# The shared key's rotation shared between VectorE and GpSimd, and a new order of roundings ahead of the attention

## The reference

```python
def mla(cq, ckv, kr, q_norm, w_uq, kv_norm, w_ukv, cos, sin):
    q = (rmsnorm(cq, q_norm) @ w_uq).reshape(B, S, ATT_HEADS, QK_DIM)          # 8 heads of 64 + 32
    q = jnp.concatenate([q[..., :NOPE_DIM], apply_rope(q[..., NOPE_DIM:], cos, sin)], axis=-1)
    q = q * QK_DIM ** -0.5
    kv = (rmsnorm(ckv, kv_norm) @ w_ukv).reshape(B, S, ATT_HEADS, NOPE_DIM + V_DIM)
    k_nope, v = kv[..., :NOPE_DIM], kv[..., NOPE_DIM:]
    k_rope = apply_rope(kr[:, :, None, :], cos, sin)                           # one key part for all heads
    k = jnp.concatenate([k_nope, jnp.broadcast_to(k_rope, (B, S, ATT_HEADS, ROPE_DIM))], axis=-1)
    ...                                                                        # softmax(q k^T) v per head

def apply_rope(x, cos, sin):
    x1, x2 = x[..., :ROPE_DIM // 2], x[..., ROPE_DIM // 2:]
    return jnp.concatenate([x1 * c - x2 * s, x2 * c + x1 * s], axis=-1)
```

## Time and profile before

| | |
|---|---|
| median of 3 runs | 1396.53 us (1396.4 to 1396.9) |
| span of the profiled execution | 1392.5 us, mean granted TensorE clock 0.994 |
| lowest run less that span | 3.9 us |
| PE busy | 1360.1 us, 98% of the span |
| DVE, ACT, POOL busy | 879.0, 662.6, 680.1 us |
| chain that ended last | 86% on PE |

### The profile page before, as it was taken

How to read it: one execution, slowest core, us unless ns; L and a number is a source line. 1 busy time by engine, 2 the same in 40 slices (tenths; PEclk the granted TensorE clock), 3 DMA queues, 4 the chain that set the end, 5 groups by cost and what they waited for, 6 DMA issues and landing times.

```text
span 1392.5 us, 19360 instructions
## 1 busy us (share of the span) xinstructions
PE 1360.1 (98%) x6940; PEld 1123.6 (81%) x6940; DVE 879.0 (63%) x1186; ACT 662.6 (48%) x1235; POOL 680.1 (49%) x540
## 2 busy tenths in 40 slices
PE   6999999999998999999999999999999999999997
PEld 5888888878885777888888888888888888878886
DVE  7125455535686777245684565566899888895284
ACT  5323232323456876445675555545444444545452
POOL 4374636347434764454567777775300443003480
PEclk9999999999999999999999999999999999999999
DMA  5221111111222000725533333435767744674251
GB/s 204 69 70 37 31 31 31 27 31 49 58 62 68 1 1 4 254 93 165 180 108 122 121 121 106 132 95 195 266 207 239 243 134 131 233 235 156 88 183 73
DMA packets 138254, 162.10 MB, mean 116 GB/s; under 512 B 16688, under 2 KB 82224, under 8 KB 138160
## 3 DMA queue, kind: packets, MB, share of 16 engines
q1 hardware_dynamic: 138160, 160.87, 36.6%
HBM read 139.86 MB, written 18.87 MB: 114 GB/s over the span
## 4 chain that ended last, share of the span: by engine, by line
PE 86%; DVE 6%; issue 3%; POOL 2%; DMA 1%; ACT 1%; SPq 0%; DVEq 0%; POOLq 0%; ACTq 0%
PE ps L50 25%; PE ps L52 24%; PE ps L51 24%; PE ps L981 4%; PE ps L1819 2%; PE ps L1860 2%; PE ps L1631 1%; PE ps L1028 1%; PE ps L1013 1%; DVE op_low L2297 1%; DVE wy_low L2303 1%; DMA k_t<-k_rope 1%; DVE w_sum L2274 1%; PE ps L1025 1%; POOL k_low L1648 0%
## 5 line engine op out<-in xcount | busy, mean ns | idle before, releaser
L1531 POOL TENSOR_TENSOR wy_low<-w_raw,wy_high 128x512 fp32r<-128x512 f32 x107 | 159.6, 1494 | 177.9 <-ACT wy_high L1474 177.8
L50 PE MATMUL ps<-wy_high,op_high 128*128 128x512 f32 x448 | 175.0, 391 | 0.8 <-DVE op_low L2297 0.4
L51 PE MATMUL ps<-wy_low,op_high 128*128 128x512 f32 x448 | 174.3, 389 | 0.0
L52 PE MATMUL ps<-wy_high,op_low 128*128 128x512 f32 x448 | 174.3, 389 | 0.0
L381 POOL TENSOR_TENSOR wx_low<-w_raw,wx_high 128x512 fp32r<-128x512 f32 (+1 forms) x64 | 83.1, 1305 | 143.1 <-ACT wx_high L501 143.1
L1474 ACT ACTIVATE wy_high<-w_raw 128x512 fp32r<-128x512 f32 x118 | 74.4, 631 | 155.0 <-PE ps L52 151.5
L1531 POOL TENSOR_TENSOR wy_low<-t_sum,wy_high 128x512 fp32r<-128x512 f32 x64 | 89.0, 1391 | 53.8 <-ACT wy_high L1474 53.6
L1531 POOL TENSOR_TENSOR wy_low<-w_sum,wy_high 128x512 fp32r<-128x512 f32 x32 | 44.4, 1388 | 130.4 <-ACT wy_high L1474 130.3
L1474 ACT ACTIVATE wy_high<-w_sum 128x512 fp32r<-128x512 f32 x80 | 50.6, 632 | 118.7 <-PE ps L52 96.6
L50 PE MATMUL ps<-h_high,wx_high 128*128 128x512 f32 (+1 forms) x256 | 102.6, 401 | 0.0
L50 PE MATMUL ps<-a_high,wy_high 128*128 128x512 f32 x256 | 100.1, 391 | 0.0
(11 more groups left out here) (292 smaller groups left out, 3512.9 us busy)
## 6 DMA issues: line engine op xcount, KB each, us to landing
w_raw<-in_w_down SPq DMA_DIRECT2D x127, 256.0 KB, 3.3
raw_more<-in_w_down SPq DMA_DIRECT2D x65, 256.0 KB, 3.5
w_raw<-in_w_up SPq DMA_DIRECT2D x64, 256.0 KB, 3.3
w_raw<-in_w_in SPq DMA_DIRECT2D x62, 256.0 KB, 2.8
w_raw<-in_w_o SPq DMA_DIRECT2D x32, 256.0 KB, 2.7
raw_more<-in_w_up SPq DMA_DIRECT2D x32, 256.0 KB, 3.3
w_raw<-in_w_ple_gate SPq DMA_DIRECT2D x32, 256.0 KB, 2.6
keep_h<-comb SPq DMA_DIRECT2D x26, 256.0 KB, 2.2
```

Of the source, the lines that this page charges most:

```text
L50: pe.matmul(out, stat_high, mov_high, start=start, stop=False)
L51: pe.matmul(out, stat_high, mov_low, start=False, stop=False)
L52: return pe.matmul(out, stat_low, mov_high, start=False, stop=stop)
L1531: pool.tensor_tensor(low_tile, tile_raw(tile), high_tile.bitcast(F32), ALU.subtract).then_inc(low_made, 1)
```

## The change

Five things change in it, all ahead of the attention.

1. The rotation of the shared key is taken from VectorE's branch `n == 12`. VectorE makes only the shuffle, into a buffer of its own (`k_swap`), ahead of its first job. GpSimd makes the four products right behind the rests of `wq`, and the sum after its second `q_rope` sum.
2. The loads of `wkv` count on their own semaphore `wkv_loaded`; VectorE waits for six loads of `p4_loaded` instead of eight, ScalarE for the two of `wkv` only when it comes to them.
3. ScalarE takes jobs 1 and 2 ahead of rounding the last latents, and jobs 4 and 5 ahead of rounding `wkv`.
4. VectorE makes the rests of the last latents at job 6 instead of ahead of job 0, and GpSimd makes the rests of `wkv` behind its first `q_rope` sum.
5. VectorE and ScalarE each wait for `q_roped` and `k_roped` before their first `v` job, and a semaphore of one count (`q_sq_added`) is merged into another.

```diff
+            k_swap = at("k_swap", [ROPE, T], F32, scratch_at + 32768)
@@ SP
-                    sp.dma_start(wkv[:, k, :]...).then_inc(p4_loaded, 16)
+                    sp.dma_start(wkv[:, k, :]...).then_inc(wkv_loaded, 16)
...
-                sp.wait_ge(k_roped, 1)
+                sp.wait_ge(k_roped, 5)
@@ GpSimd
                 for k in range(2):
                     latent_weight_low("wq", wq, wq_high, wq_low, k)
-                for k in range(2):
-                    latent_weight_low("wkv", wkv, wkv_high, wkv_low, k)
+                pool.wait_ge(p4_loaded, 16 * 6)
+                pool.wait_ge(rope_step, 1)
+                for g in range(2):
+                    pool.tensor_tensor(k_rope[:, HALVES[g]], k_rope[:, HALVES[g]], cos[0:ROPE, :], ALU.mult).then_inc(k_roped, 1)
+                    pool.tensor_tensor(k_swap[:, HALVES[g]], k_swap[:, HALVES[g]], sin[0:ROPE, :], ALU.mult).then_inc(k_roped, 1)
...
                         pool.tensor_tensor(out, out, buf, ALU.add).then_inc(q_roped, 1)
+                        if steps_of == 1:
+                            for k in range(2):
+                                latent_weight_low("wkv", wkv, wkv_high, wkv_low, k)
+                        if steps_of == 2:
+                            pool.wait_ge(k_roped, 4)
+                            pool.tensor_tensor(k_rope[:, :], k_rope[:, :], k_swap[:, :], ALU.add).then_inc(k_roped, 1)
@@ ScalarE
-                for n in range(4, 6):
-                    latent_high(n)
-                act.wait_ge(p4_loaded, 16 * 8)
-                for k in range(2):
-                    latent_weight_high(wkv, wkv_high, k)
                 for n, (kind, m, h) in enumerate(jobs):
+                    if n == 3:
+                        latent_high(4)
+                        latent_high(5)
+                    if n == 6:
+                        act.wait_ge(wkv_loaded, 16 * 2)
+                        for k in range(2):
+                            latent_weight_high(wkv, wkv_high, k)
+                    if (kind, m) == ("v", 1):
+                        act.wait_ge(q_roped, 4)
+                        act.wait_ge(k_roped, 5)
@@ VectorE
-                step, roped = 0, 0
-                for n in range(4, 6):
-                    latent_low(n)
-                dve.wait_ge(p4_loaded, 16 * 8)
+                step, roped = 1, 0
+                dve.wait_ge(lat_made, 8)
+                dve.stream_shuffle(k_swap[:, :], k_rope[:, :], swap).then_inc(rope_step, 1)
+                dve.wait_ge(p4_loaded, 16 * 6)
                 for n, (kind, m, h) in enumerate(jobs):
+                    if n == 6:
+                        latent_low(4)
+                        latent_low(5)
+                    if (kind, m) == ("v", 0):
+                        dve.wait_ge(q_roped, 4)
+                        dve.wait_ge(k_roped, 5)
...
-                        if n == 12:
-                            ...
-                            dve.stream_shuffle(kt, kr, swap).then_inc(rope_step, 1)
-                            ...
-                            dve.tensor_tensor(kr, kr, kt, ALU.add).then_inc(k_roped, 1)
```

More of the change, by code:

```diff
@@ L267, in front_of @@
             (lgain_loaded, latent_squared, sums_full, l_mean_made, l_rstd_made, normed, p4_loaded, rope_step, q_roped, k_roped,
-             job_full, q_sq_added, diag_made, spread_full) = (sem(top, "p4_" + n) for n in (
+             job_full, diag_made, spread_full, wkv_loaded) = (sem(top, "p4_" + n) for n in (
                  "lgain_loaded", "squared", "sums_full", "mean", "rstd", "normed", "loaded", "rope_step", "q_roped",
-                 "k_roped", "full", "q_sq_added", "diag", "spread"))
+                 "k_roped", "full", "diag", "spread", "wkv_loaded"))
             (k_made, k_sum_made, total_made, q_made, level_full, level_read, q_decayed, kt_full, kt_made,
@@ L356, in sp_front @@
                 for k in range(2):
-                    sp.dma_start(wkv[:, k, :].rearrange("p (h c) -> p h c", h=AH), ukv[:, :, k, :]).then_inc(p4_loaded, 16)
+                    sp.dma_start(wkv[:, k, :].rearrange("p (h c) -> p h c", h=AH), ukv[:, :, k, :]).then_inc(wkv_loaded, 16)
                 for m in range(2):
@@ L470, in pool_front @@
                             pool.tensor_tensor(latent_sq[:, 0, :], latent_sq[:, 0, :], latent_sq[:, 1, :],
-                                               ALU.add).then_inc(q_sq_added, 1)
+                                               ALU.add).then_inc(latent_squared, 1)
                         if (j, slot) == (3, ("lv", 2, 1)):
@@ L485, in pool_front @@
                         out, buf = q_rope[:, m, HALVES[h]], rot[:, HALVES[h]]
-                        pool.wait_ge(rope_step, 2 * steps_of)
+                        pool.wait_ge(rope_step, 2 * steps_of + 1)
                         pool.wait_ge(job_dve, readers(jobs.index((kind, m, h)))[0])
                         pool.tensor_tensor(out, out, buf, ALU.add).then_inc(q_roped, 1)
+                        if steps_of == 1:
[4 more added lines that the diff above has]
+                            pool.tensor_tensor(k_rope[:, :], k_rope[:, :], k_swap[:, :], ALU.add).then_inc(k_roped, 1)
             def act_front(act):
@@ L883, in dve_front @@
                                           None, ALU.mult).then_inc(job_dve, 1)
-                        if n == 12:
-                            dve.wait_ge(q_roped, 4)
-                            dve.wait_ge(lat_made, 8)
-                            kr, kt = k_rope[:, :], rot[0:ROPE, :]
-                            dve.stream_shuffle(kt, kr, swap).then_inc(rope_step, 1)
-                            dve.wait_ge(rope_step, step + 1)
-                            for g in range(2):
-                                dve.tensor_tensor(kr[:, HALVES[g]], kr[:, HALVES[g]], cos[0:ROPE, :],
-                                                  ALU.mult).then_inc(rope_step, 1)
-                                dve.tensor_tensor(kt[:, HALVES[g]], kt[:, HALVES[g]], sin[0:ROPE, :],
-                                                  ALU.mult).then_inc(rope_step, 1)
-                            dve.wait_ge(rope_step, step + 5)
-                            dve.tensor_tensor(kr, kr, kt, ALU.add).then_inc(k_roped, 1)
                     elif m % 2 == 0:
@@ L1032, in latent_sums @@
                     pe.wait_ge(state_made, 12 * (HH - 1))
-                    pe.wait_ge(q_sq_added, 1)
-                    pe.wait_ge(latent_squared, 3)
+                    pe.wait_ge(latent_squared, 4)
                     for n, m in ((0, 0), (1, 2)):
```

## The result

| | before | after |
|---|---|---|
| median | 1394.55 us (1392.99 to 1397.42, 22 runs) | 1398.17 us (1395.40 to 1402.09, 22 runs) |
| span of the profiled execution, clock | 1392.5 us, 0.994 | 1394.0 us, 0.994 |

The ratio is 1.0027 [1.0019, 1.0035], so the change costs 3.6 us. The forecast, 1398.4, lies beside the measured 1398.2, but for a reason that is not its merit: it was counted from a median of 1396.53, and beside the changed kernel the kernel before ran at 1394.55. What was forecast was +1.9 us, and with 0.64 a difference that cannot be told from none; what came is +3.6 and slower, clear of zero.

A forecast was written before the change was run, and what follows sets the result against it. The prediction took the landing of the shared key's DMA as ending the stage ahead of the attention. Landing +1.4 and clock +0.5 gave +1.9 on 1396.53, so 1398.4 us; range 1394.6 to 1401.0.

The forecast's parts named there:

- Q: End of GpSimd's fourth q_rope sum, which releases the last four q_t DMAs; forecast at 416.9, 3.2 us later than before.
- VectorE's rests of the latents ask at 405.7; the first is in at 406.9: At job 6, VectorE's rests wait for GpSimd's rests of wkv; the first wait is 1.2 of 5.1 us forecast in all.
- My bounds: Range for Q: 412.7 with no waiting of VectorE for GpSimd, 417.4 with all of it and products of 1.30 us.
- The wrong-if of the prediction: Signs of error: fourth q_rope sum ending before 415, VectorE's products at 0.68 beside GpSimd, or attention starting before 427.
- Key ready at 411.5, its DMA right behind the gains: Key's sum done on GpSimd at 411.5; its DMA waits in SP's queue until Q + 3.54, at 420.4, 1.0 later.
- The landing: End of the key's DMA, behind which the attention starts: +1.4 us taken, between +1.0 (same 8.05 transfer) and 2.5 later.
- the 0.7 us that I had called free: Before the key's DMA: of a 2.1 us gap, only some 0.7 us of DMA work was free, giving a landing 2.5 later.
- The clock: PE stands before the attention, so the half clock falls on its first scores and transposes: 0.5 us taken, bounds nothing to 1.5.
- one amount of work, and the clock falls on the attention: Rival: DMAs are one amount of work from Q on, +2.5, and the clock costs +1.5 on the attention: 1400.5; chance 0.20.
- The transfer hides it: Rival: the key's landing moves by under 0.5 us either way, absorbed by queue and slack: 1396.5; chance 0.08.
- nothing collides: Rival: GpSimd's new instructions don't delay VectorE; Q = 412.7, landing 3.1 or 1.7 earlier: 1394.1; chance 0.06.
- they share the port: Rival: GpSimd and VectorE share rather than exclude, each L875 costing 0.49 more; Q = 415.0, 1396.4; chance 0.14.

The follow-up runs named there:

- parts 2 to 4: Kernel before with parts 2 to 4 of the change alone, the key's rotation left on VectorE behind the first k job: 1394.73 us, ratio 0.9996.
- the late kernel: Changed kernel with VectorE's two rests of the latents made to wait for GpSimd's first rest of wkv: 1400.38 us, ratio 1.0042.
- two others with the same DMAs: Changed kernel with GpSimd's rests of wkv waiting for VectorE's rests of the latents, ratio 1.0035; changed kernel run once more, ratio 1.0020.
- 30 matmuls more: Changed kernel with 30 unused matmuls added on PE between the last v job and the attention: 1399.50 us, ratio 1.0036.

## Why the prediction was right, and where it was wrong

The time came out within the range, and what the forecast says GpSimd does to VectorE is what the rows show. That the time came within 0.2 is luck all the same: the difference was 1.7 larger than forecast, and the base from which it was counted 2.0 too high.

- **Q, +3.2 forecast, +1.5 measured.** The mechanism was right for single instructions: L896 took 1.46, 1.54 and 1.32 in three of four places (forecast 1.2 to 1.8), and GpSimd worked without a gap, even until Q. The step that failed is "VectorE's rests of the latents ask at 405.7; the first is in at 406.9": they asked 0.12 behind GpSimd and were let in, so VectorE waited 2.3 us in all and not 5.1. That the other order exists, with Q 4.6 later than before, I had not seen. My bounds (412.7 to 417.4) do not reach it (418.4 in the frame of the profile before). Two readings were off a little: the L875 ended 0.55 and not 0.60 behind GpSimd's first rest (401.50; 401.45 is the start of the second), and the lower bound keeps the 0.5 of waiting that the kernel before has. The wrong-if of the prediction ("the fourth sum ends before 415") came true in the profile's own time, 413.7; counted from the common zero it ended at 415.3 in the frame of the profile before.
- **Key ready at 411.5, its DMA right behind the gains.** Ready 18.5 behind the zero, forecast 17.6; issued at Q + 3.65, forecast Q + 3.54. Right.
- **The landing, +1.4 forecast, +1.6 measured**, from two errors that cancel. "From there it took 8.05" was taken as the nearer row; the transfer took 10.06. Landing less Q is 13.7 in before, after, parts 2 to 4 and the late kernel, 13.8 and 14.0 in two others with the same DMAs, whether the key went 5.6 or 3.7 behind Q. So from Q on the DMAs are one amount of work, which was the rival, without even the 0.7 us that I had called free. With the forecast's own Q this would have been +3.2. What I left out of that amount is `w_raw`, behind the key in the queue: with 30 matmuls more, more of it went ahead, and the landing came 15.2 behind Q. And the speed "205 to 213 GB/s" is not in those rows (158, 176, 213); 205 stands in other windows of that profile.
- **The clock, +0.5 forecast, +1.7 measured.** The place and the cause were right, the size was not. "The PE part of some 3 us of that chain twice" counted too short a stretch: the clock stayed at 0.50 for 5 us after the start, and the first four scores alone took 3.75 instead of 1.96.
- The case that came about is the rival "one amount of work, and the clock falls on the attention" (+2.5 and +1.5 forecast, +1.6 and +1.7 measured, 0.20 of the chance); the forecast with 0.52 had it at half its size.
- "The transfer hides it", "nothing collides" and "they share the port" are out: S follows the landing by 0.13 to 0.14 in every kernel in which the key ends the stage, and rests that wait end 0.55 behind GpSimd's instructions, not at a slower rate of their own.
- ScalarE's order and the own semaphore cost nothing, as forecast: parts 2 to 4 alone bring S forward by 0.9. The new waits ahead of the `v` copies were not run apart; in the changed profile these copies start at 415.5 and 417.6, behind Q at 413.7, so they were met.

## What to carry to other kernels

When a value is made earlier, follow its transfer through the queue: here it gained nothing while loads that nobody needed yet were issued ahead of it. Count the landing of the last of several DMAs by the bytes that move from the moment at which they were released, with those of the loads issued right behind it, and not by its own duration in a row. Before two engines that use the port pair are given more work side by side, look for instructions that ask within a few tenths of a microsecond of one another: a single wait, placed so that the one on the path goes first, fixes the order, though here no median got better by it. And where an idle stretch of TensorE moves up to the start of the next stage, count the half clock over the whole first part of that stage.

## What had not been expected of the hardware

- The start of a GpSimd instruction in the profile is not the moment at which it holds the port: VectorE came 0.12 to 0.14 us after it and went first in four profiles, and came 0.13 to 0.14 us after it and was held for over 4 us in three.
- A waiting VectorE instruction can be passed over at the end of a GpSimd instruction when the next one is ready (1.22 us and then 1.25 more in the late kernel). By the Trainium skill (the same page and section) the lock is held for one whole instruction; here the one that waited was not always next, and was held for two or three.
- One and the same 1 MiB transfer took 6.96, 8.05, 10.06 and 11.56 us, by what stood ahead of it in the queue and by how much of the loads issued behind it moved first (0.20, 0.46, 0.45 and 0.76 MB).
- GpSimd's products on 32 partitions took the 1.28 us of 128 partitions, and its sum on 1,024 elements 2.40.
- PE stood from 429.5 to 432.2 in the kernel with 30 matmuls more, and the clock read 0.50 from 433 on, in the middle of the scores.
